# State space layer's input projection: seven block products in place of eight, with sums on VectorE and GpSimd and two weight ring slots in that stage

## The reference

```python
u_l, g_l = jnp.split(h_lat @ w_in, 2, axis=-1)     # w_in: 1024 x 4096
u_c, g_c = jnp.split(h_ctx @ w_in, 2, axis=-1)     # u: 2048 wide, g of the context is not used
...
bu = jnp.einsum('btgs,gps->btgp', u_chunk.astype(jnp.complex64), b_bar)
_, xs = lax.associative_scan(_ssm_combine, (a, bu), axis=1)
...
y = jnp.einsum('btgp,gsp->btgs', xs, cmat).real
...
ya, yb = jnp.split(y @ w_glu + b_glu, 2, axis=-1)
return ((ya * jax.nn.sigmoid(yb)) * jax.nn.silu(g)) @ w_out
```

## Time and profile before

| | us |
|---|---|
| time, median of 3 runs | 1574.27 |
| lowest and highest run | 1570.85, 1575.98 |
| span of the profiled execution, first to last instruction | 1571.2 |
| TensorE busy in the span | 1503.4 |
| VectorE busy | 872.9 |
| ScalarE busy | 402.3 |
| GpSimd busy | 565.2 |

### The profile page before, as it was taken

How to read it: one execution, slowest core, us unless ns; L and a number is a source line. 1 busy time by engine, 2 the same in 40 slices (tenths; PEclk the granted TensorE clock), 3 DMA queues, 4 the chain that set the end, 5 groups by cost and what they waited for, 6 DMA issues and landing times.

```text
span 1571.2 us, 25477 instructions
## 1 busy us (share of the span) xinstructions
PE 1503.4 (96%) x10192; PEld 1129.3 (72%) x10192; DVE 872.9 (56%) x1745; ACT 402.3 (26%) x956; POOL 565.2 (36%) x412
## 2 busy tenths in 40 slices
PE   4999989999999999999998999999999999999998
PEld 3455555666655558898877888887788874688887
DVE  5979944554578978378466321243543422265642
ACT  1222243333311222322233011001223550232210
POOL 4013340000002314101002977773496301477774
PEclk9999999999999999999999999999999999999999
DMA  9856771050286646747666455445544133455441
GB/s 332 221 173 194 242 237 45 3 159 14 100 262 228 202 174 180 273 166 287 251 252 260 159 195 182 161 163 185 191 167 146 70 108 107 131 179 164 168 150 68
DMA packets 172605, 272.99 MB, mean 174 GB/s; under 512 B 51405, under 2 KB 85304, under 8 KB 171208
## 3 DMA queue, kind: packets, MB, share of 16 engines
q1 hardware_dynamic: 146096, 201.08, 38.1%
q0 software_dynamic: 16512, 42.49, 8.4%
q10 hardware_dynamic: 9880, 27.78, 4.8%
HBM read 228.26 MB, written 42.99 MB: 173 GB/s over the span
## 4 chain that ended last, share of the span: by engine, by line
PE 88%; DVE 5%; DMA 3%; issue 2%; ACT 2%; POOL 0%; DVEq 0%; ACTq 0%; POOLq 0%
PE bank L499 82%; PE bank L502 6%; DMA memory<-in_w_mod 1%; DMA memory<-mc_scratch 1%; DVE memory L2417 1%; DVE memory L2418 1%; DVE memory L2424 0%; DVE memory L2421 0%; DMA memory<-in_s_log_dt 0%; DVE memory L2574 0%; ACT memory L1514 0%; ACT memory L1386 0%; ACT memory L1738 0%; DVE memory L2445 0%; DVE memory L2444 0%
## 5 line engine op out<-in xcount | busy, mean ns | idle before, releaser
L499 PE MATMUL bank<-memory 128*128 128x256 f32 (+8 forms) x9244 | 1404.7, 355 | 40.4 <-issue 8.5
L499 PEld LDWEIGHTS bank<-memory 128*128 128x128 f32 (+4 forms) x9244 | 1022.3, 166 | 378.1 <-issue 250.1
L2783 POOL DMA_DIRECT2D mc_scratch<-memory x32 | 28.0, 874 | 505.5 <-DVE memory L2138 447.7
L502 PEld LDWEIGHTS bank<-memory 128*128 128x128 f32 (+1 forms) x948 | 109.3, 142 | 59.4 <-issue 33.6
L502 PE MATMUL bank<-memory 128*128 128x128 f32 (+1 forms) x948 | 125.9, 277 | 23.5 <-ACT memory L1358 8.6
L2822 POOL TENSOR_TENSOR memory<-memory 128x1024 f32<-128x1024 f32 (+1 forms) x34 | 80.9, 2378 | 143.5 <-PE bank L499 96.2
L2808 POOL DMA_DIRECT2D memory<-mc_scratch x32 | 17.3, 541 | 189.7 <-PE bank L499 189.7
L2824 POOL TENSOR_TENSOR memory<-memory 128x1024 f32<-128x1024 f32 (+1 forms) x34 | 80.9, 2380 | 2.7
L2789 POOL DMA_DIRECT2D k_scratch<-memory x128 | 76.2, 629 | 14.5 <-ACT memory L1431 14.1
L2827 POOL TENSOR_TENSOR memory<-memory 128x1024 f32<-128x1024 f32 (+1 forms) x34 | 80.0, 2353 | 2.7
L2825 POOL TENSOR_TENSOR memory<-memory 128x1024 f32<-128x1024 f32 (+1 forms) x34 | 80.4, 2366 | 0.0
(11 more groups left out here) (305 smaller groups left out, 1284.3 us busy)
## 6 DMA issues: line engine op xcount, KB each, us to landing
memory<-in_s_w_glu SPq DMA_DIRECT2D x32, 1024.0 KB, 7.5
memory<-in_w_mod SPq DMA_DIRECT2D x12, 2048.0 KB, 14.1
memory<-in_w_ffn_up SPq DMA_DIRECT2D x22, 1024.0 KB, 6.9
memory<-in_w_in SPq DMA_DIRECT2D x10, 2048.0 KB, 8.0
mc_scratch<-memory POOLq DMA_DIRECT2D x32, 512.0 KB, 4.5
mb_scratch<-memory ACTq DMA_DIRECT2D x32, 512.0 KB, 3.7
memory<-mb_scratch SPq DMA_DIRECT2D x32, 512.0 KB, 7.3
memory<-mc_scratch POOLq DMA_DIRECT2D x32, 512.0 KB, 6.5
```

What stands on the lines that cost most here:

```text
L499: return nc.tensor.matmul(o, l, r, start=start, stop=stop, skip_group_check=free)
L502: return nc.tensor.transpose(o, i, ident[0:n, 0:n])
L2783: pool.dma_start(mc_dram[u], over(mc[:, u % 3, GS:GS + 1], (144, 8), (1, P))).then_inc(*S.up("mc_out%d" % (u % 3), u, by=16))
```

## The change

A product of two matrices cut into 2 by 2 blocks can be made with seven block products instead of eight, if sums of the blocks are made first and sums of the products afterwards. The change does this for `u`, in eight pieces: for each block `q` and each half `n` of the tokens (256 tokens as two groups of 128, 1024 channels as two of 512, 512 columns as two of 256).

- **Left sums.** VectorE makes four sums of blocks of `hT` for each `n`, eight operations of 128 x 512 in all, right after `modulated(1, 1)`; they serve all four `q`. They lie in a ring slot that is kept for them ("held" loads, which load nothing), so the weights of the stage go through two slots.
- **Weight sums.** GpSimd makes four sums of 128 x 1024 for each `q`: three at once (`u_weight_sums`), the fourth (`u_last_weight_sum`) when the products 5 are done, since it takes the first one's place.
- **Products.** `u_product(q, n, i)` makes one of the seven. Products 1, 2 and 4 take `hT` itself, 64 tokens at a time in two halves of the array (8 matrix products); products 3, 5, 6 and 7 take the sums, with 128 tokens at once (4 matrix products).
- **Joining.** ScalarE copies seven parts out (`u_parts`), and GpSimd adds five times 128 x 256 for each `q` and `n` (`u_joined`), before `u_turned` may run. `by_channel` is four copies of 64 partitions in place of one.
- **Moved.** The four operations of the residual (`x1_scaled`) go from VectorE to GpSimd (`residuals_scaled`). VectorE's copy of the powers waits for a product too. The order around the products, and SP's order, are written anew.

```diff
-S5IN_ORDER = (4, "u0", 5, "u1", "u2", "u3", 6, 7)
+S5IN_ORDER = (4, "u0", "held0", 5, "u1", "held1", "u2", "u3", "held2", 6, 7)
...
+                for k in range(4):
+                    for rows, tokens in zip(whole if len(left[k]) == 1 else halves, left[k]):
+                        last = mm(o[rows], tokens, right[:, k, :], start and k == 0, i in (2, 3, 4, 6) and k == 3, True)
...
+            def u_first(q):
+
+                u_products(q, 0, 1, 5)
+                u_products(q, 1, 5)
+                u_products(q, 0, 7, 6)
...
-            u_tile(2, 0)
+            u_first(2)
+            u_products(2, 0, 2, 3, 4)
             additions(12, 16)
             direct(0, 1)
-            u_tile(2, 1)
-            outputs(0, 3)
-            u_tile(2, 2)
-            outputs(3, 6)
-            u_tile(2, 3)
-            outputs(6, 8)
+            u_products(2, 1, 1, 7)
+            outputs(0, 1)
+            u_products(2, 1, 6)
+            outputs(1, 2)
+            u_products(2, 1, 2)
+            outputs(2, 3)
+            u_products(2, 1, 3)
+            outputs(3, 4)
+            u_products(2, 1, 4)
+            outputs(4, 6)
             direct(1, 0)
+            outputs(6, 7)
             u_turned(2)
-            additions(16, 19)
-            u_tile(3, 0)
-            additions(19, 22)
-            u_tile(3, 1)
-            additions(22, 24)
+            outputs(7, 8)
+            additions(16, 20)
+            u_first(3)
+            u_products(3, 0, 2, 3, 4)
+            additions(20, 24)
             direct(1, 1)
...
+            for n in range(2):
+                q11, q12, q21, q22 = (over(hT[:, k0, 2 * n + half:2 * n + half + 1], (2 * T, 4), (4, 2), (L, NC)) for half in range(2) for k0 in (0, 4))
+                left_sums(u_sums[:, :, :, n * P:(n + 1) * P].rearrange("p i k (m c) -> p i k m c", m=2), q11, q12, q21, q22,
+                          "u_sum", ((n, 1), (n, 3), (n, 2), (n, 4)))
             for u in range(NU - LATE + 1, NU):
                 unit(u)
-            dve.wait_ge(*S.at("lnbc0"))
-            for t in range(2):
-                dve.wait_ge(*S.at("x1", t))
-                link(tt(x[:, t, :], xr[:, t, :], lnbc0[:, 0, :], ALU.mult))
-                tt(x[:, t, :], x[:, t, :], lnbc0[:, 1, :], ALU.add).then_inc(*S.up("x1_scaled", t))
...
             dve.wait_ge(*S.at("kern_mm", NU // 2 - 1))
+            dve.wait_ge(*S.at("product", (("u", 0, 1), 6)))
...
+                if q == 0:
+                    pool.wait_ge(*S.at("res0", (1, 3)))
+                elif q == 1:
+                    for u in (NU - 2, NU - 1):
+                        pool.wait_ge(*S.at("mbt_out%d" % (u % 2), u))
+                else:
+                    pool.wait_ge(*S.at("product", (("u", q - 1, 1), 4)))
+                nc.gpsimd.tensor_tensor(t1, b12, b11, ALU.subtract).then_inc(*S.up("w_sum", (("u", q), 1)))
...
+            def residuals_scaled():
+                pool.wait_ge(*S.at("mb", NU - 1))
...
             for half in range(2):
                 for u in range(16 * half, 16 * half + 16):
+                    if u == NU - LATE:
+                        u_weight_sums(0)
+                    elif u == NU - LATE + 1:
+                        u_last_weight_sum(0)
+                    elif u == NU - LATE + 2:
+                        u_joined(0, 0, 1, 2, 5, 3, 4)
                     c_store(u)
...
                 for kp in (8 * half + 6, 8 * half + 7):
+                    if kp == NU // 2 - 1:
+                        u_joined(0, 1, 1, 2, 5, 3, 4)
+                        residuals_scaled()
                     taps_store(kp)
...
             mb_load(15, 19)
+            t_load(1, 0)
             ring(("s5in", 6))
-            t_load(1, 0)
-            ring(("s5in", 7))
             t_load(1, 1)
             mb_load(19, 27)
             t_load(2, 0)
+            ring(("s5in", 7))
             t_load(2, 1)
```

More of the change, by code:

```diff
@@ L403, in build @@
                 parts = [w_in1[:, :, par * 1024 + q * 256:par * 1024 + (q + 1) * 256] for par in range(2)]
-                load(("s5u", q), None, (2, KD, 256), ("u_mm", (q, 3)), parts)
+                load(("s5u", q), None, (2, KD, 256), ("product", (("u", q, 1), 4)), parts)
+        held = {load_no[("held", n)] % SLOTS for n in range(3)}
+        assert len(held) == 1
+        u_sums = ring[:, held.pop(), 0:4096].rearrange("p (i k t) -> p i k t", i=4, k=4)
         first_glu = len(loads)
@@ L832, in gate_tile @@
                 last.then_inc(*S.up("s5in_mm", f))
[L834 to L844, removed]
+            u_banks = {}
@@ new lines, in u_product @@
+            def u_product(q, n, i):
+                b11, t3, b21, b22 = up_quarters(weights(pe, ("s5u", q), (2, KD, 256)))
+                t1, t2, t4 = weight_sums(("u", q))
+                lo, hi = slice(0, T), slice(T, 2 * T)
+                if i == (5 if n else 1):
+                    u_banks[q, n] = [bank(pe, ("u", q, n, 0), [("u_part", (q, n, 3))], next(spare))]
+                    if n:
+                        spare.keep()
+                elif i == 7:
+                    u_banks[q, n].append(bank(pe, ("u", q, n, 1), [("u_part", (q, n, 4))], next(spare)))
+                b = u_banks[q, n]
+                whole, halves = [slice(0, P)], [slice(0, 64), slice(64, P)]
+                raw = lambda half, k0: [[over(hT[:, k0 + k, 4 * p + 2 * n + half:4 * p + 2 * n + half + 1], (L, NC)) for p in range(2)] for k in range(4)]
+                summed = lambda s: [[u_sums[:, s, k, n * P:(n + 1) * P]] for k in range(4)]
+                if i in (1, 2):
+                    o, left, right = b[0][:, lo], raw(0, 0 if i == 1 else 4), b11 if i == 1 else b21
+                elif i in (5, 3):
+                    o, left, right = b[0][:, hi], summed(0 if i == 5 else 3), t1 if i == 5 else b22
+                elif i == 7:
+                    o, left, right = b[1][:, lo], summed(2), t3
+                elif i == 6:
+                    o, left, right = b[1][:, hi], summed(1), t2
+                else:
+                    o, left, right = b[1][:, lo], raw(1, 4), t4
+                if i in (5, 6, 7, 3):
+                    pe.wait_ge(*S.at("u_sum", (n, {5: 1, 6: 2, 7: 3, 3: 4}[i])))
+                if i in (5, 6, 7, 4):
+                    pe.wait_ge(*S.at("w_sum", (("u", q), {5: 1, 6: 2, 7: 3, 4: 4}[i])))
+                if i in (2, 4):
+                    pe.wait_ge(*S.at("u_part", (q, n, 6 if i == 4 else 1 if n else 5)))
+                start = i == 7 or i == (5 if n else 1)
+                for k in range(4):
+                    for rows, tokens in zip(whole if len(left[k]) == 1 else halves, left[k]):
+                        last = mm(o[rows], tokens, right[:, k, :], start and k == 0, i in (2, 3, 4, 6) and k == 3, True)
+                last.then_inc(*S.up("product", (("u", q, n), i)))
+                if n and i == 4:
+                    spare.give()
@@ L935, in _ @@
             additions(7, 8)
-            for jp in range(4):
-                u_tile(1, jp)
+            u_first(1)
+            u_products(1, 0, 2, 3, 4)
+            u_products(1, 1, 1, 7, 6, 2, 3, 4)
             direct(0, 0)
@@ L2946, in _ @@
             ring(("s5in", 5))
-            ring(("s5u", 1))
             for u in (29, 30, 31):
```

212 lines of the change are left out of this document (164 added, 48 removed), and 2 rows, old and new, of the table SHARED.

## The result

The changed kernel takes 1625.72 us (median of 4 runs, 1624.89 to 1627.8), the kernel before 1573.57 in the same comparison: the ratio is 1.0335 (95% interval 1.0322 to 1.0349). That is slower, as forecast, but by 52 us in place of 19, and outside the range.

The account below looks back on a forecast made before the run. TensorE, busy 96% of the span, was taken as the bound. Savings, waits, clock and shape changes summed to +18.7 us on 1571.2, 1589.9, plus 3.1 for the median: 1593 us, range 1568 to 1607.

Parts of the forecast that it names:

- the hold: VectorE's two-input operations beside GpSimd's sums: one gets in per sum, each full sum costing VectorE 2.14 us, a join 0.58.
- block 1's wait: TensorE waits 3.5 us (bounds 0 and 6) behind block 1's first additions, as GpSimd's work lengthens recurrence 0.
- one term of 1.0: Joins ahead of the other turnings, and tables of `outputs`: 1.0 us in all.
- the clock: TensorE's lower granted clock after a long wait: 1.7 us each, behind the pole tables' wait and that for Table 19.
- a change of shape: On TensorE between products of different shape: 0.18 us each, 34 more of them, 6.1 us in all.
- The start: GpSimd's first three weight sums hold VectorE ahead of the scaling TensorE waits for: 1.5 us later.
- Table 19: Stored table ahead of `additions(19)`, block 2, landing late behind 2 MB of weights: wait 6 and clock 1.7, 7.7 us.
- table 23: Stored table asked for after `additions(20)`, nothing ahead in the queue: wait of 1.5 us.
- table 27: Stored table covered by two additions and a gate, with `s5in` 7 newly ahead: 0 to 4.8, taken as 1.5 us.
- Rival A: Joins and residual sums fall into VectorE's idle time, so it isn't held where it matters: 1578 us, chance 0.13.
- rival B: No hold where it matters and free changes of shape, so all 13.8 us saved show: 1566 us, chance 0.10.
- rival C: 2 MB weights push tables 19, 23 and 27 to the longest landing, 24.6 us for 10.7: 1607 us, chance 0.10.

Follow-up runs that it names:

- gaps: Changed kernel, but VectorE waits for its own last operation at the end of each recurrence step: 1613.13 us, ratio 1.0239.
- short_all: Changed kernel with all of GpSimd's weight sums and joins cut to one column, order and semaphores kept: 1628.8 us, ratio 1.0351.
- fourth_early: Changed kernel with block 1's fourth weight sum given its own place, made ahead of recurrence 0: 1617.17 us, ratio 1.0285.
- tables_first: Changed kernel with GpSimd issuing loads of stored tables ahead of the joins of blocks 2 and 3: 1613.23 us, ratio 1.0263.
- late2g: Changed kernel, block 0 as eight products, residual on VectorE, left sums later, loads, joins and additions reordered, pauses in recurrences, joins on GpSimd: 1580.11 us, ratio 1.0045.

## Why the prediction was wrong in size

**The step that failed** is that of the hold: "VectorE gets one operation in for each GpSimd sum, and each such sum costs it 2.14 us". The earlier trace rows show it for one short row of sums, where GpSimd was already adding when VectorE began and VectorE waits for its own results on the way. I took it as the rule and asked only what GpSimd's additions cost VectorE, never what a recurrence without a pause costs GpSimd. So block 1's wait was priced as a longer recurrence (14.3 us more, wait 3.5). Its first part took 25.6 us in place of 21.7, not 36:

```profile
677.25 0.42 DVE L2541 TENSOR_TENSOR memory<-memory 128x256 f32<-128x256 f32 x1 [17.55 <-ACT memory L1718]
...
702.87 0.14 DVE L2561 COPY memory<-memory 1x1 f32<-1x1 f32 x1
```

VectorE hardly paid, GpSimd did, with 9.70 us of TensorE, and the wait of 3.5 behind block 1's first additions did not come. And the loads behind the joins in GpSimd's queue shared one term of 1.0, without a working; they cost 8.29 and 8.42. The three are 26.4 us, and 8.6 of clock follow them. That in the recurrences the lack of a pause is the cause is shown by gaps and short_all together; that a row of operations without one always shuts GpSimd out is not (see what is still open). That order and place of the shut-out operation carry it to TensorE, is shown by fourth_early and tables_first. The Trainium skill ("SBUF — State Buffer", section "SBUF: two separate sides") says that of a VectorE operation with two inputs in on-chip memory and a GpSimd operation that reads it, the one that starts first has the shared ports for its whole instruction and the other blocks. The held rows agree (2.83 us beside 2.80); that a run of instructions keeps the other out from one to the next, 14.59 us for one column, the page does not say.

**The second mis-sized term** is the clock: 3.4 us more than before, behind two waits; measured 18.0 more, behind eight. The row for it was there, but not applied to each new wait. (It was also read a little high: TensorE is busy for 1.40 of the first 2 us, so that the loss before is 1.5 and not 1.7.)

**Point by point.** TensorE's own saving: 8.7 for 7.7; a change of shape costs some 0.20 us for 0.18 (eight instructions of 128x256 begin 1.92 to 1.94 us ahead of the next shape, 1.73 at their own pace). The start: 1.2 us later for 1.5 (the 1.90 us scaling starts later behind the held `unit(28)`), but with 1.7 of clock. L2368, L2489 now, took 2.65 us in place of 0.81 beside GpSimd's sums, so this one-input operation was held too; the 2.2 that the forecast had for that case did not come of it. `lam_tables`: 659.6 for 656.3, its mechanism right. From 608.8 on the hold cost VectorE 16.4 us for 16.5, with the powers at 2.45 to 2.73 us from 643.7 to 653.9; what was mis-sized is the left sums, 8.2 us in place of 5.4, most of that with no sum of GpSimd beside them (its next began at 608.19):

```profile
600.58 1.10 DVE L2428 TENSOR_TENSOR memory<-memory 128x512 f32<-128x512 f32 x1 [0.23 <-DVE memory L2040]
...
607.83 1.08 DVE L2433 TENSOR_TENSOR memory<-memory 128x512 f32<-128x512 f32 x1
...
643.72 2.47 DVE L2156 TENSOR_TENSOR memory<-memory 128x256 f32<-128x256 f32 x1
...
651.20 2.73 DVE L2153 TENSOR_TENSOR memory<-memory 128x512 f32<-128x512 f32 x1
...
659.55 0.14 DVE L2523 COPY memory<-memory 1x1 f32<-1x1 f32 x1
```

The wait for it is 4.13 and 2.8 of clock, 6.9 for 8.5, since TensorE came later itself: `additions(0)` at 647.9 in place of 642.6, where I had taken no change. That was 3.23 us for a unit that the left sums and the hold made late, its clock of 1.7, and the clock of the start. Table 19: 4.44 and 3.0, 7.4 for 7.7, right; table 23: 2.60 for 1.5; table 27: 1.66 for 1.5. Rival A, no hold where it matters, is refuted by the powers' rows; rival B, by the waits; rival C, longer loads, had 8.2 us for tables 19 and 23, which took 4.44 and 2.60, and does not explain the three long waits.

**Still open**: what decides, in one execution and not the next, that the units let block 0's joins in. The two outcomes are 5.7 and 21.4 us for the same five joins, though VectorE runs `unit(29)` without a pause in both: in the changed kernel's profile its operations there took 1.2 us in place of 0.69, one join between each and the next. Open too is the last 6.8 us of late2g over the kernel before, spread over waits of at most 3.21 us.

## What to carry to other kernels

Where two engines exclude each other, as VectorE and GpSimd did here, price it both ways: what the added work costs the engine that is there, and how long that engine may go on without a pause. A wait for its own result between steps of a long chain cost VectorE 0.13 us a step here and let the other in; the chain then pays for what it lets in (36.6 us in place of 25.6), so place the pauses where the other's work is needed soon. And before adding an operation to a queue, look at which load stands behind it; a saving of a few microseconds on a full TensorE is gone with two or three waits, and here eight of nine were paid again at the lower clock.

## What the runs showed of the hardware

- GpSimd's two-operand sum of one column took 14.59 us beside a recurrence of VectorE and 0.18 alone: the time was set by when it got in, not by its length.
- Pauses of VectorE at each of seven steps brought a 128x1024 sum there from 16.74 to 2.45 us.
- The granted clock was at its lower level for 3.5 to 6.2 us of work behind eight waits of 2.35 to 9.70 us, 1.7 to 3.0 us each, and not behind one of 2.60.
